# Raw key pages scored on TensorE inside the attention's projection, and the router's embedding tiles one place up

## The reference, cut to what matters

```python
def nsa_compress(kv_cmp, pos_w):
    ...
    w = jax.nn.softmax(pos_w.astype(jnp.float32), axis=1).astype(kv_cmp.dtype)
    kvc = jnp.einsum('bnlckd,clk->bnckd', blocks, w)
    return kvc[:, :, 0], kvc[:, :, 1]
...
    s_c = jnp.einsum('btkrd,bnkd->btkrn', q, kc)
```

## Time and profile before

| what | value |
|---|---|
| median of the runs | 1052.1 us |
| the profiled execution's own time | 1056.3 us |
| its span, first to last instruction | 1054.2 us |
| PE, DVE, ACT, POOL busy | 999.7, 491.0, 334.2, 187.8 us |
| mean granted clock of PE | 0.968 |
| moved by DMA | 343.20 MB, mean 326 GB/s |

### The profile page before, as it was taken

One profiled execution on the slowest core, in us unless ns is written; L12 is line 12 of the kernel. 1 busy time (PEld: TensorE's weight loads), 2 busy tenths in 40 slices (PEclk: granted clock), 3 DMA queues, 4 the chain that ended last, 5 costly groups with the idle time before them and its releaser, 6 DMA issues. The chain is left out here.

```text
span 1054.2 us, 14961 instructions
## 1 busy us (share of the span) xinstructions
PE 999.7 (95%) x5177; PEld 624.7 (59%) x5177; DVE 491.0 (47%) x1422; ACT 334.2 (32%) x875; POOL 187.8 (18%) x201
## 2 busy tenths in 40 slices
PE   8999999899999999998899977979999999999897
PEld 6888776788744444443678854544875444444366
DVE  2889797871611111111379986671153111112046
ACT  3212888710451111110340013572044211112134
POOL 0000016311120000000345542441103000000033
PEclk9999999999899999999999986998998999999999
DMA  9963787779669999999727995959985999999974
GB/s 324 315 214 130 225 271 248 250 240 404 272 273 427 427 427 426 426 426 428 302 93 271 377 352 168 305 169 368 427 335 214 426 427 426 425 427 426 426 301 205
DMA packets 90144, 343.20 MB, mean 326 GB/s; under 512 B 15890, under 2 KB 53906, under 8 KB 73170
## 3 DMA queue, kind: packets, MB, share of 16 engines
q1 hardware_dynamic: 80074, 319.48, 78.2%
q10 hardware_dynamic: 7688, 18.39, 4.9%
q0 software_dynamic: 2304, 4.33, 1.2%
HBM read 331.56 MB, written 23.04 MB: 336 GB/s over the span
## 5 line engine op out<-in xcount | busy, mean ns | idle before, releaser
L1522 DVE TENSOR_TENSOR gates_and_hidden<-bank,gates_and_hidden 128x512 f32<-128x512 f32 x16 | 11.1, 692 | 311.4 <-PE bank L1173 311.4
L1173 PE MATMUL bank<-expert_ring,x_packed 128*64 128x512 f32 x320 | 118.6, 607 | 0.0
L1154 PE MATMUL bank<-expert_ring,x_packed 128*64 128x512 f32 x416 | 112.7, 593 | 0.9 <-DMA expert_ring<-in_moe_w_gate 0.9
L559 PE MATMUL ss<-xT,expert_ring 128*128 128x264 f32 x384 | 89.5, 393 | 4.4 <-DMA expert_ring<-in_ssd_w_in 4.4
L559 PEld LDWEIGHTS ss<-xT,expert_ring 128*128 128x128 f32 x384 | 73.1, 193 | 18.3 <-DMA xT<-in_xT 4.4
L1154 PEld LDWEIGHTS bank<-expert_ring,x_packed 128*64 128x64 f32 x416 | 36.6, 137 | 73.3 <-issue 73.3
L1383 POOL DMA_INDIRECT x_rows_packed<-x_rows,slot_token_int x16 | 16.4, 1023 | 339.3 <-DVE gates_and_hidden L1487 293.4
L1517 DVE TENSOR_TENSOR acc<-acc,bank 128x264 f32<-128x264 f32 x128 | 55.0, 429 | 39.1 <-PE bank L1210 37.5
L1765 PE MATMUL bank<-xT,expert_ring 128*128 128x264 f32 (+1 forms) x324 | 72.5, 386 | 0.3 <-PEq L1006 0.3
L1195 PE MATMUL bank<-expert_ring,gates_and_hidden 128*64 128x512 f32 x256 | 70.8, 595 | 1.4 <-ACT gates_and_hidden L1344 1.4
L1765 PEld LDWEIGHTS bank<-xT,expert_ring 128*128 128x128 f32 (+1 forms) x324 | 60.2, 187 | 12.5 <-issue 1.0
(11 more groups left out here) (417 smaller groups left out, 1840.3 us busy)
## 6 DMA issues: line engine op xcount, KB each, us to landing
expert_ring<-in_moe_w_gate SPq DMA_DIRECT2D x26, 2048.0 KB, 19.8
expert_ring<-in_moe_w_up SPq DMA_DIRECT2D x18, 2048.0 KB, 20.0
expert_ring<-in_moe_w_down SPq DMA_DIRECT2D x16, 2048.0 KB, 20.0
expert_ring<-in_ssd_w_in SPq DMA_DIRECT2D x9, 2048.0 KB, 8.7
expert_ring_b<-in_moe_w_gate SPq DMA_DIRECT2D x6, 2048.0 KB, 17.8
expert_ring_c<-in_moe_w_up SPq DMA_DIRECT2D x6, 2048.0 KB, 22.5
expert_ring_d<-in_moe_w_up SPq DMA_DIRECT2D x6, 2048.0 KB, 21.0
expert_ring_c<-in_moe_w_down SPq DMA_DIRECT2D x6, 2048.0 KB, 22.5
```

Source lines behind the costliest of these rows:

```text
L559: last = mm(pt[m % 4][:, 0:T], wc[:, k, ((m - 1) % 4) * P:((m - 1) % 4 + 1) * P], xT[:, k, :], start=k == 0, stop=k == KD - 1)
L1154: last = mm(hb[0][s * CAP:(s + 1) * CAP, :], xg[:, k, s * CAP:(s + 1) * CAP], unit(6 * i + s)[:, k * FF:(k + 1) * FF], start=k == 0, stop= ...
L1173: last = mm(hb[1][s * CAP:(s + 1) * CAP, :], xg[:, k, s * CAP:(s + 1) * CAP], unit(6 * i + 2 + s)[:, k * FF:(k + 1) * FF], start=k == 0, s ...
```

## The change

Keys are no longer compressed ahead of the score. The pages of compressed and selected keys are stored side by side (`k_pages`), loaded in eight blocks of eight pages of 256 KB, and PE scores both raw (`dec_keys`, 16 products of 256 columns a block). DVE weights the raw scores of the compressed branch by position and sums them per block (`key_half`), once for each half of the past. Values alone are compressed (`vcmp_pages`, transfers of 128 KB, six half buffers), all on DVE; POOL's multiplies go. The eight key blocks stand between projection tiles 8 and 15. The gates' tile moves to place 16, and tiles from 8 on use two banks. All pages and page numbers are on SP's queue; ACT issues weight chunks alone. A new buffer `ring_e` holds every fourth key block. The window's bias is taken from the last 512 columns of the past's bias. The orders of the attention's small steps, of the output weights and of the units for the next tail change. In both tails the embedding's tiles 2 to 6 stand one step earlier, ACT empties tile 0 ahead of its last two copies, and `keep_busy(1)` issues one product that nothing reads.

```diff
+        def cmp_buffer(b):
+            c, half = (2, 0, 1)[b % 6 // 2], b % 2
+            return ring[:, 0, c * CH + half * (CH // 2):c * CH + (half + 1) * (CH // 2)].rearrange("p (n c t) -> p n c t", n=NPG, c=2)
+
+        cmp_landed = lambda b: 2 * 16 * NPG * (b // 6 + 1)
...
-                        load_unit(sp, L, 3 + 2 * L, unit(3 + 2 * L))
+                        if L == 0:
+                            load_unit(sp, L, 3, unit(3))
...
                             load_cmp(sp, 0, page)
+                            load_cmp(sp, 1, page)
                             sp.wait_ge(sc_done, n8 + 8 * NP2)
                             for c in range(2):
                                 load_chunk(sp, c, I["nsa_w_in"][c])
+                            page = {n: page_number(sp, n) for n in range(2 * NPG, 4 * NPG)}
                             sp.wait_ge(e_done, 4)
-                            load_cmp(sp, 1, page)
+                            load_cmp(sp, 2, page)
+                            load_cmp(sp, 3, page)
...
+                        def keep_busy(n):
+                            for _ in range(n):
+                                mm(hb[1][:, 0:T], ones[:], xT[:, 0, :], start=True, stop=True)
+
                         for c in range(6):
                             turn_x(c)
                         project(0)
                         project(1)
+                        project(2)
 
...
-                        project(2)
+                        project(3)
+                        keep_busy(1)
...
-                            project(3 + i)
+                            project(4 + i)
...
-                        project(5)
+                        project(6)
...
                         turn_rows(0)
-                        project(6)
                         project(7)
...
+                            if c == 3:
+                                take_projected(0)
+                        for m in range(1, 7):
                             take_projected(m)
...
-                        take_projected(6)
...
+            kv_buf = [ring[:, 0, n * CH:(n + 1) * CH] for n in range(3)] + chunk[0:2] + [ring_e[:]]
+            KV_SLOT = (5, 0, 1, 2, 5, 0, 1, 2, 5, 0, 1, 2, 4, 3, 5, 0)
+            NKEY, KWIN, VAL = 8, 8, 10
+            kv_dmas = lambda j: 8 if j < NKEY else 4 if j in (KWIN, KWIN + 1, VAL + 2, VAL + 5) else 16
...
+            GATES, nchunk = KD + 8, (KD + KVT) // 4
+            KEYS_AT = {8: (0, 1), 9: (2,), 10: (3,), 12: (4,), 13: (5,), 14: (6,), 15: (7,)}
+            tile_bank = lambda m: m if m < KD else 2 + m % 2
...
+                    table, n = ("k_pages", 2) if j < NKEY else ("vsel_pages", 4)
+                    for i, page in enumerate(pages[j]):
+                        src = I[table][bass.ds(page, 1)].rearrange("a p c -> (a p) c")
+                        sp.dma_start(kv_buf[s][:, i * CH // (4 * n):(i + 1) * CH // (4 * n)], src).then_inc(ld_kv[s], 16)
...
+            def read_pages(sp, j):
+
+                if j < NKEY:
+                    t, first, n = j % 2, 2 * (j // 2), 2
+                else:
+                    t, first, n = (j - VAL) // 3, 4 * ((j - VAL) % 3), 4
+                pages[j] = [page_number(sp, (2 * g + t) * NPG + first + q) for g in range(4) for q in range(n)]
...
+                    page = {n: page_number(sp, n) for n in range(4 * NPG, 6 * NPG)}
+                    load_cmp(sp, 4, page)
+                    load_cmp(sp, 5, page)
...
+                                   (wgates, "nsa_w_gates")):
+                        sp.dma_start(dst[:], I[n]).then_inc(ld_nc, 16)
+                    page = {n: page_number(sp, n) for n in range(6 * NPG, 8 * NPG)}
                     sp.wait_ge(c_used, 2)
-                    load_cmp(sp, 4, page)
                     load_cmp(sp, 6, page)
+                    load_cmp(sp, 7, page)
+                    read_pages(sp, 0)
+                    load_kv(sp, 0)
+                    for j in range(1, 4):
+                        read_pages(sp, j)
+                        sp.wait_ge(c_used, 2 * j + 2)
+                        load_kv(sp, j)
+                    for j in range(4, VAL + 2):
+                        if j < NKEY or j >= VAL:
+                            read_pages(sp, j)
+                        sp.wait_ge(kv_used, j - 3)
+                        load_kv(sp, j)
+                    sp.wait_ge(tile_done, d0 + GATES)
+                    load_kv(sp, VAL + 2)
+                    read_pages(sp, VAL + 3)
+                    sp.wait_ge(tile_done, d0 + NT)
...
+                    read_pages(sp, VAL + 4)
+                    sp.wait_ge(kv_used, KWIN + 1)
+                    load_kv(sp, VAL + 4)
+                    sp.wait_ge(kv_used, KWIN + 2)
+                    load_kv(sp, VAL + 5)
+                    sp.wait_ge(kv_used, VAL + 1)
+                    sp.dma_start(kv_buf[1], I["nsa_w_out"][0]).then_inc(ld_wo[0], 16)
+                    sp.wait_ge(kv_used, VAL + 2)
+                    load_unit(sp, 1, 7, kv_buf[2])
+                    sp.wait_ge(kv_used, VAL + 3)
                     load_unit(sp, 1, 0, kv_buf[4])
-                    for n in (1, 2):
+                    sp.wait_ge(kv_used, VAL + 5)
+                    sp.dma_start(kv_buf[5], I["nsa_w_out"][1]).then_inc(ld_wo[1], 16)
+                    load_unit(sp, 1, 5, kv_buf[3])
+                    sp.wait_ge(kv_used, VAL + 6)
+                    load_unit(sp, 1, 3, kv_buf[0])
...
-                    for b in range(1, DB):
-                        pool.wait_ge(ld_cmp[cmp_slot(b)], 16 * NPG * (b // 3 + 1))
-                        for a in range(2, 4):
-                            cmp_multiply(nc.gpsimd, b, a).then_inc(c_mult, 1)
...
+                    def tile(m):
+                        if m >= KD:
+                            pe.wait_ge(tile_taken, t0 + m - 1)
...
                     def dec_keys(j):
+                        t, pp, a, s = j % 2, j // 2 % 2, j // 4, KV_SLOT[j]
...
+                        k5 = kv_buf[s].rearrange("p (g q c t) -> p g q c t", g=4, q=2, c=4)
+                        for kind, bk in enumerate((pt[4 + a], dp[a])):
+                            for p in range(2):
+                                for g in range(4):
+                                    q0 = (2 * g + t) * P + 32 * g
+                                    last = mm(bk[32 * g:32 * g + 32, pp * 256:(pp + 1) * 256], qbd[:, p, q0:q0 + 32], k5[:, g, :, 2 * kind + p, :],
...
+                    for m in range(NT):
+                        tile(m)
+                        for j in KEYS_AT.get(m, ()):
+                            dec_keys(j)
+                        if m == GATES:
+                            score(0)
+                        elif m == GATES + 2:
+                            cmp_scores()
+                            turn_gates()
                     score(1)
+                    turn_new_values()
...
-                        if pair <= 2:
-                            dec_keys(pair)
-                        if pair == 4:
-                            dec_keys(3)
...
-                    def load_batch(b):
-                        for n in range(b * NPG, (b + 1) * NPG):
-                            page[n] = page_number(act, n)
-                        act.wait_ge(c_used, b - 2)
-                        load_cmp(act, b, page)
...
+                        if m == 4:
+                            act.wait_ge(row_max, 1)
+                            A_(pos_row[:], pos_row[:], ACT.Exp, bias=pos_stat[:, 0:1], accum_out=pos_stat[:, 1:2]).then_inc(row_exp, 1)
...
+                    def key_half(a):
+                        dve.wait_ge(kv_used, 4 * a + 4)
+                        raw = sw[:, 0:512].rearrange("p (n l) -> p n l", l=BLK)
+                        V.tensor_tensor(raw, pt[4 + a][:].rearrange("p (n l) -> p n l", l=BLK), pos_row[:].unsqueeze(1).to_broadcast([P, NBP // 2, BLK]), ALU.mult).then_inc(kc_read, 1)
+                        dve.wait_ge(kc_read, a + 1)
...
+                    compress(0)
+                    compress(1)
+                    dve.wait_ge(ld_nc, 16 * 12)
+                    V.tensor_reduce(pos_stat[:, 0:1], pos_row[:], AX.X, ALU.max, negate=True).then_inc(row_max, 1)
+                    for b in range(2, DB):
                         compress(b)
+                    spread_queries()
+                    dve.wait_ge(row_exp, 1)
+                    dve_step(dve, V.reciprocal(pos_stat[:, 1:2], pos_stat[:, 1:2]))
+                    key_half(0)
+                    prompt_blocks()
+                    take_half(0)
+                    key_half(1)
+                    take_half(1)
```

More of the change, by code:

```diff
@@ L1024, in _ @@
                         if L == 0:
-                            page = [page_number(sp, n) for n in range(2 * NPG)]
+                            page = {n: page_number(sp, n) for n in range(2 * NPG)}
                         if L == 1:
@@ L1693, in _ @@
-                    read_pages(6)
-                    sp.wait_ge(c_used, 4)
```

(36 more changed lines are left out.)

304 lines of the change are left out of this document (113 added, 191 removed).

## The result

The changed kernel takes 1102.3 us (median of four runs, 1100.2 to 1103.8) against 1051.6 beside it (four runs, 1046.0 to 1054.4): ratio 1.0508, interval 1.0466 to 1.0550, slower by some 50 us. The profiled execution took 1102.4 us with a span of 1100.7; the one of before had 1054.2, so the two traces differ by +46.5.

The account below looks back on a forecast made before the run. SP's queue, issuing page reads and transfers, was taken to bound the kernel: later loop start +45.2, loop -7.5, routers -2, sum +35.7 us added to the 1052.1 median gave 1088 us, range 1066 to 1108.

Parts of the forecast that it names:

- What bounds it: Projection: SP's queue issues 96 reads and 96 transfers at 0.53 us and 12 constants, 108 us in all.
- 4 of backlog: SP's queue up to the last key block: 4 us added because issues stretch when transfers queue up, bounds 0 and 10.
- The first key block: Behind projection tile 8: PE idles from about 582 to 606, released by DVE's spread queries.
- The last: Eighth key block ahead of the loop: its pages land at 667.0, then PE needs 1.9 us for the block.
- The value pages in the loop: Issued on SP at 17 us per 16, done near 735, before the value products need them near 749: hidden.
- What follows it: PE from the last key pages' landing to the loop: block, five tiles, scores and turns of new values, 27.6 us.
- The loop: Attention loop loses four key blocks, 8.7 us, but DVE is late next: -7.5 us, bounds -4 and -10.
- The routers: Router tiles of both layers, reordered: -1 us a layer, -2 in all, bounds -7 and +1; gathered rows bind.
- The high end: Whole kernel: backlog 10, half clock 9, loop -4, routers +1, together +57 us, 1109.
- SP ahead of PE: Rival at the first key block: pages and queries ready by 582, PE sets the pace, 1039 us; chance 0.05.
- Transfers as the pace: Rival up to the loop: 28.4 MB at 313 GB/s take 91 us, +10, 1062 us; chance 0.04.
- The unused product: Rival in the routers: the product holds no clock, +1 in place of -2 us, inside the range; no separate chance.

Follow-up runs that it names:

- The run with one number: Changed kernel reading one page number per key block instead of eight, all eight transfers taking that page: 1077.5 us, ratio 1.0286.
- the run with all blocks last: Changed kernel with all eight key blocks and the prompt's block scores behind the last projection tile: 1080.2 us, ratio 1.0298.
- unused products: Changed kernel with ten unused products in PE's wait for the new values just ahead of the loop: 1102.3 us, ratio 1.0533.
- the versions that mend SP's queue: Changed kernel with half the key blocks on ACT's queue, 1091.2 us; three combinations also moving constants to ACT and key blocks later, 1068.7, 1060.3, 1057.3 us.
- ACT's help: Changed kernel with key blocks 1, 3, 5 and 7 read and issued by ACT between its tiles: 1091.2 us, ratio 1.0425.

## Why the prediction was right, point by point

**What bounds it: right.** SP's queue does, at about half a microsecond a read and a transfer. The run with one number and the run with all blocks last show it from both sides. SP's program took 115.7 us up to the last key issue; forecast were 107.6 and 4 of backlog, 111.6. A read takes 0.56 to 0.58 with its gap, not 0.53, and sixteen value transfers took 9.09 us, not 8.5.

**The first key block: right.** Forecast 55.6 us behind the projection's first tile (606 - 550.4), released by the queries; measured 56.2, by the queries. A batch of values takes DVE 4.65 us, 4.6 forecast. **The last: nearly.** Forecast 116.6, measured 119.8. **The value pages in the loop: hidden, right.** PE waits there for DVE and ACT alone, 1.6 us at the longest.

**What follows it: 27.6 forecast, 36.7 measured.** This is the term of the sum that was mis-sized most. The 4.84 us for the new values are missing in it. I had counted turns, not who fills them: the change put DVE's copy behind the scaling that needs ACT's exponentials, and ACT's queue reaches these only behind the last tile and a table load. The prediction doesn't price that edit at all. The run with DVE's order changed back shows the wait go to 1.08. Most of the rest is the clock: the last block at 3.49 us and not 1.9, the two tiles behind the prompt's scores 9.08 and not 7.2.

**The loop: -7.5 forecast, +1.0 measured**, outside my bounds of -4 and -10. The key products did leave (761 products of PE became 698), but PE's busy time stayed, 80.80 to 80.46, at a granted clock of 0.85 in place of 0.94. Lengths and clocks of the loop go together, but not closely. Of the eleven traces with the new loop the two at 0.85 and 0.87 (changed, unused products) take 90.5 and 90.2 us; the nine at 0.88 to 0.94 take 85.6 (blocks last) to 87.7. The three traces with the loop of before take 88.1 to 90.9. At a clock of 0.94 or 0.95 it is 85.6 and 86.4 new against 88.1 and 89.6: 2 to 4 us shorter, at most about half of what I took. In the run with DVE's order PE's busy time is 7.1 us less than in the profile of before, its idle time 3.9 more (86.43 - 73.75 against 89.59 - 80.83), so some of the blocks had stood in time that PE now spends waiting.

```profile
691.59:778.02 86.43, 73.75 (x698) 41.35 (x698) 49.65 (x175) 47.74 (x168) 32.70 (x64) 0.94 0.67 241
```

The blocks had also kept PE busy at the loop's start, where the lower clock level now stands behind the waits (the first 14 us run at 0.50, in the profile of before at 0.87); why it rises sooner in one run than in another stays open.

**The routers: -2 forecast, -2.2 measured** by the run with this part alone (interval -4.7 to +0.6). The reason I gave is not shown: with the new order all twelve traces have stretches of 24.5 to 26.4 us and gain more there than the 3.4 I allowed, against a profile of before that was slow there.

**The sum.** On the traces: +57.5 + 1.0 - 9.9 - 2.1 = +46.5, forecast +35.7. The miss of 3.2 at the last key block, 9.1 behind it and 8.5 in the loop make 20.8; the routers' 7.9 more and the experts' 2.1 hid half of it. That was luck: I had not forecast it, and the run with the router part alone doesn't give it. By the medians the result stands 14 us over the 1088. The profile of before stood 4.2 above its median, and I added the difference as if it were the same in every stage; by the estimate above, most of it lay in the two router stretches that the change touched. The high end held 9 us for the lower clock level. Some 7 were spent, by the traces, on the last block, on two of the five tiles and in the loop.

**The rivals.** SP ahead of PE: no, first key block at 599.73 and not 576 or so. Transfers as the pace: not here, at 0.82 of the engines, but in the versions that mend SP's queue the transfers are at their limit. The Trainium skill ("DMA: Bandwidth & Descriptors", section "Rules for kernel authors") says that spreading transfers over queues doesn't help bandwidth and only saves the sequencer's issue time. The runs agree: ACT's help brought 280 to some 400 GB/s because issue had been the limit, and nothing beyond. The unused product: without it the time is the same (1.0482 against 1.0508, intervals overlapping).

## What to carry to other kernels

Count what one queue must issue before a deadline, the reads of indices too: here a page costs its queue as much for its number as for its transfer, and 96 of each are over 100 us that no busy time shows. An engine's work taken away gains nothing if its data then comes through one queue ahead of an engine with a fixed order, or if the engine that takes the work over has no time to spare; put blocks that may be late behind all work that doesn't need them. And when a change reorders small steps ahead of a loop, price the order by who waits for whom, and look at more than one execution of before if its clock is low.

## What was not expected of the hardware

With two queues the core's transfers, most of them 256 KB pages, ran at 389 to 404 GB/s with a DMA share of 1.03 to 1.05, and the last key block took some 20 us from issue to landing; the output projection's 2 MB transfers reach 426. Taking 8.7 us of products out of the loop left PE's busy time as it was in the changed kernel, 80.46 us: what was left ran at a lower granted clock. And the mean clock of the kernel before differs between executions, 0.967 to 0.982 over 52, with 1042 to 1059 us.
